# A two-layer diffusion block on one core: token tiles first in the queue, and a bias split into high and low part

## What is computed

```python
for l in range(DEPTH):                      # DEPTH = 2
    mod_l = split(silu(c) @ ada_w[l] + ada_b[l], 6)        # adaLN, latent; mod_c alike from c_ctx
    pl = modulate(rms_norm(xl, norm1_g[l]), mod_l[0], mod_l[1]) @ w_in[l]
    ml, mc = token_mixing(pl, pc, ...)      # pooling, neighbourhood attention, gMLP, latent attention
    xl = xl + mod_l[2] * (ml @ w_out[l])
    hl = modulate(rms_norm(xl, norm2_g[l]), mod_l[3], mod_l[4])
    xl = xl + mod_l[5] * grouped_moe(hl, ...)               # 16 experts, top 2
...
# neighbourhood attention
s_win = q . k * scale + bias                # bias from the learned table rpb, by row and column distance
s_win = where(valid, s_win, -1e30)
p = softmax(concat([s_win, s_ctx]))
```

## Time and profile before

| | us |
|---|---|
| runs: median of 3 (lowest, highest) | 913.67 (911.79, 914.56) |
| the profiled execution | 915.42 |
| its span, first to last instruction | 913.6 |
| TensorE busy, of the span | 836.8 |
| VectorE busy | 548.3 |
| ScalarE busy | 466.5 |
| GpSimd busy | 76.0 |

### The profile page before, as it was taken

One profiled execution on the slowest core, in us unless ns is written; L12 is line 12 of the kernel. 1 busy time (PEld: TensorE's weight loads), 2 busy tenths in 40 slices (PEclk: granted clock), 3 DMA queues, 4 the chain that ended last, 5 costly groups with the idle time before them and its releaser, 6 DMA issues. The chain is left out here.

```text
span 913.6 us, 15179 instructions
## 1 busy us (share of the span) xinstructions
PE 836.8 (92%) x6042; PEld 708.6 (78%) x6042; DVE 548.3 (60%) x807; ACT 466.5 (51%) x648; POOL 76.0 (8%) x103
## 2 busy tenths in 40 slices
PE   2989999999999789999999848999999799999985
PEld 2758967756787579999999835898669599999974
DVE  1263233249732777778778736662485668888854
ACT  1362221159721646566666525751673667676734
POOL 0103000520004000000000040302102000000000
PEclk9789999999999699999999975999999799999996
DMA  9796798984113037888988869952345159999901
GB/s 322 234 286 141 249 325 271 305 273 144 62 46 93 1 117 257 297 288 307 307 289 291 267 226 346 256 182 93 107 127 161 37 162 351 353 332 327 359 9 46
DMA packets 169122, 197.49 MB, mean 216 GB/s; under 512 B 15538, under 2 KB 156252, under 8 KB 169052
## 3 DMA queue, kind: packets, MB, share of 16 engines
q1 hardware_dynamic: 164400, 180.70, 62.4%
q10 hardware_dynamic: 3500, 11.64, 3.3%
q0 software_dynamic: 1152, 4.19, 1.4%
HBM read 187.09 MB, written 9.44 MB: 215 GB/s over the span
## 5 line engine op out<-in xcount | busy, mean ns | idle before, releaser
L2162 DVE TENSOR_TENSOR w_lo<-raw,w_hi 128x2048 fp32r<-128x2048 f32 x96 | 219.6, 2290 | 38.0 <-ACT w_hi L1071 37.4
L1071 ACT ACTIVATE w_hi<-raw 128x2048 fp32r<-128x2048 f32 x96 | 183.6, 1913 | 67.7 <-PE bank L1216 58.7
L1214 PE MATMUL bank<-w_hi,xg_hi 128*128 128x256 f32 x384 | 111.7, 291 | 3.1 <-DVE xg_lo L2323 2.5
L1215 PE MATMUL bank<-w_lo,xg_hi 128*128 128x256 f32 x384 | 109.3, 285 | 0.0
L1216 PE MATMUL bank<-w_hi,xg_lo 128*128 128x256 f32 x384 | 109.2, 284 | 0.0
L1214 PE MATMUL bank<-h_hi,w_hi 128*128 128x512 f32 (+2 forms) x288 | 103.9, 361 | 4.9 <-DVE h_lo L1934 4.0
L1215 PE MATMUL bank<-h_lo,w_hi 128*128 128x512 f32 (+2 forms) x288 | 101.5, 353 | 0.0
L1216 PE MATMUL bank<-h_hi,w_lo 128*128 128x512 f32 (+2 forms) x288 | 101.3, 352 | 0.0
L1214 PEld LDWEIGHTS bank<-w_hi,xg_hi 128*128 128x128 f32 x384 | 74.1, 193 | 3.4 <-issue 3.4
L1215 PEld LDWEIGHTS bank<-w_lo,xg_hi 128*128 128x128 f32 x384 | 74.4, 194 | 0.0
L1216 PEld LDWEIGHTS bank<-w_hi,xg_lo 128*128 128x128 f32 x384 | 74.2, 193 | 0.0
(11 more groups left out here) (302 smaller groups left out, 1598.2 us busy)
## 6 DMA issues: line engine op xcount, KB each, us to landing
raw<-in_ada_w SPq DMA_DIRECT2D x48, 1024.0 KB, 9.7
raw<-in_moe_w_gate SPq DMA_DIRECT2D x32, 1024.0 KB, 6.0
raw<-in_moe_w_up SPq DMA_DIRECT2D x32, 1024.0 KB, 6.3
raw<-in_moe_w_down SPq DMA_DIRECT2D x32, 1024.0 KB, 5.5
raw<-in_w_in SPq DMA_DIRECT2D x14, 1024.0 KB, 11.5
raw<-in_w_out SPq DMA_DIRECT2D x8, 1024.0 KB, 6.5
y_rows<-y_sb ACTq DMA_DIRECT2D x16, 512.0 KB, 4.8
na_bias<-in_na_rpb SPq DMA_DIRECT2D x4, 384.0 KB, 7.5
```

Of the source, the lines that this page charges most:

```text
L1071: act.activation(w_hi[slot][:, :, :], raw[q][:, :, :], ACT.Copy).then_inc(split_hi, 1)
L1214: pe.matmul(dst, w_hi_, x_hi_, start=first, stop=False)
L1215: pe.matmul(dst, w_hi_, x_lo_, start=False, stop=False)
L2162: dve.tensor_tensor(w_lo[slot][:, :, :], raw[q][:, :, :], w_hi[slot][:, :, :].bitcast(F32), ALU.subtract).then_inc(split_lo, 1)
```

## The change

Three things at the start, one in the attention.

1. The token tiles are issued by SyncE ahead of the first weight block. ScalarE's queue holds only the first constants, now 258 columns (identity, ones, epsilon), ahead of the vectors. Cosine and sine come with the other constants, later, in SyncE's queue; VectorE waits for these (`s_const`) before the first use.
2. The adaLN blocks with places 6 and 7 go to two buffers of their own, `ada_first`, in the room of `h_hi`, and don't wait for a slot.
3. The first modulation no longer stands ahead of the column sums, but between their two halves.
4. ScalarE copies the reversing matrix to fp32r (`flip`) and `na_bias` to its high part `bias_hi`, after block 6 of each layer. VectorE writes the low part `bias_lo` in the room of `na_bias`, ahead of block 7. TensorE adds the bias with two one-pass products, high and low part. `bias_hi` lies over `w_uq`, `w_uqs` and `sgu_wt`, so the copy waits for `s_go`. For this, `sgu_wt` moves ahead of `w_ukv`.

```diff
-N_FIRST = C_FLIP
+N_FIRST = C_COS
...
+        flip = sb("flip", [P, P], F32R)
+        bias_at = at[0]
         w_uq = sb("w_uq", [P, 2, HEADS * QK])
         w_uqs = sb("w_uqs", [P, 2, HEADS, ROPE])
+        sgu_wt = sb("sgu_wt", [P, 4, P])
         w_ukv = sb("w_ukv", [P, 4 * P])
         sgu_w_at = at[0]
         sgu_w = sb("sgu_w", [P, 4, P])
-        sgu_wt = sb("sgu_wt", [P, 4, P])
+        bias_hi = nc.alloc_sbuf_tensor_at("bias_hi", [P, HEADS, 6, GRID], F32R, offset=bias_at)
+        bias_lo = nc.alloc_sbuf_tensor_at("bias_lo", [P, HEADS, 6, GRID], F32R, offset=at[0])
         na_bias = sb("na_bias", [P, HEADS, 6, GRID])
...
+        ada_first = [nc.alloc_sbuf_tensor_at(f"ada_first{i}", [P, KC, BW], F32, offset=h_at + 4 * KC * BW * i) for i in range(2)]
...
+        def raw_of(l, r):
+
+            n = raw_index(l, r)
+            return ada_first[n - RAW] if RAW <= n < 8 else raw[n % RAW]
...
-                if p >= RAW:
+                if p >= (RAW if l else 8):
                     bl, br = ORDER[l][p - RAW]
...
-                sp.dma_start(raw[n % RAW][:, :, 0:w],
+                sp.dma_start(raw_of(bl, r)[:, :, 0:w],
...
+            for t in range(4):
+                sp.dma_start(x_tok[t][:, :], a["x" if t < 2 else "ctx"][(t % 2) * P:(t % 2 + 1) * P, :]).then_inc(s_xin, 16)
             for p in range(RAW):
                 load_block(0, p)
...
+            act.dma_start(const[:, 0:N_FIRST], a["const"][:, 0:N_FIRST]).then_inc(s_ident, 16)
             act.dma_start(raw_vec[0][0:112, :], a["vec0"]).then_inc(s_vecin, 16)
             act.dma_start(raw_vec[1][0:N_VEC - 112, :], a["vec1"]).then_inc(s_vecin, 16)
-            act.dma_start(const[:, 0:N_FIRST], a["const"][:, 0:N_FIRST]).then_inc(s_ident, 16)
-            for t in range(4):
-                act.dma_start(x_tok[t][:, :], a["x" if t < 2 else "ctx"][(t % 2) * P:(t % 2 + 1) * P, :]).then_inc(s_xin, 16)
...
+                    if n == 6:
+                        act.wait_ge(s_bias, 3 * l + 1)
+                        act.wait_ge(s_go, l + 1)
+                        act.activation(flip[:, :], const[:, C_FLIP:C_FLIP + P], ACT.Copy)
+                        act.activation(bias_hi[:, :, :, :], na_bias[:, :, :, :], ACT.Copy).then_inc(s_bias, 1)
...
                     for k in range(KC):
+                        if k == KC // 2:
+                            pe.wait_ge(s_cact, 1)
+                            modulate(0, bank[START_BANK[0]])
                         pe.wait_ge(n_sqa if k % 2 == 0 else n_sqd, k // 2 + 1)
...
-                    modulate(0, bank[START_BANK[0]])
...
-                            pe.matmul(dst[hd][:, 0:S], const[:, C_FLIP:C_FLIP + P],
-                                      na_bias[:, 2 * pair + hd, s:s + 4, :].rearrange("p r c -> p (r c)"),
-                                      start=False, stop=True, skip_group_check=True).then_inc(t_sc, 1)
+                            for part in (bias_hi, bias_lo):
+                                ins = pe.matmul(dst[hd][:, 0:S], flip[:, :], part[:, 2 * pair + hd, s:s + 4, :].rearrange("p r c -> p (r c)"),
+                                                start=False, stop=(part is bias_lo), skip_group_check=True)
+                            ins.then_inc(t_sc, 1)
...
-                pe.wait_ge(s_bias, l + 1)
+                pe.wait_ge(s_bias, 3 * l + 3)
...
+                    if n == 7:
+                        dve.wait_ge(s_bias, 3 * l + 2)
+                        dve.tensor_tensor(bias_lo[:, :, :, :], na_bias[:, :, :, :], bias_hi[:, :, :, :].bitcast(F32), ALU.subtract).then_inc(s_bias, 1)
...
                     if n == 1:
+                        if l == 0:
+                            dve.wait_ge(s_const, 16)
                         dve.tensor_copy(k_rope[rr, :], bank[3][0:ROPE, :])
```

More of the change, by code:

```diff
@@ L1242, in modulate @@
                     for g, (l, j) in enumerate(blocks):
-                        ins = pe.matmul(dst[32 * g:32 * g + 32, 0:BW], c_pad[:, k, :], raw[raw_index(l, j) % RAW][:, k, :],
+                        ins = pe.matmul(dst[32 * g:32 * g + 32, 0:BW], c_pad[:, k, :], raw_of(l, j)[:, k, :],
                                         start=(k == 0), stop=(k == KC - 1))
@@ L1321, in _ @@
             pe.transpose(bank[0][:, 112:N_VEC], raw_vec[1][0:N_VEC - 112, :], ident[0:N_VEC - 112, 0:N_VEC - 112]).then_inc(s_vt, 1)
-            pe.wait_ge(s_cact, 1)
             for l in range(DEPTH):
```

## The result

| | before | after |
|---|---|---|
| first comparison: median of 5 and 5 runs | 912.94 (911.12 to 914.56) | 908.83 (907.40 to 909.81) |
| the profiled execution | 915.42 | 908.22 |
| its span | 913.6 | 906.4 |
| its mean granted clock | 0.938 | 0.936 |

The ratio is 0.9939, with a 95% interval of 0.9914 to 0.9964. So the change makes the kernel faster, by 4.1 us in this comparison. Run twice more, beside other runs of the kernel before, the same kernel gave 0.9964 (0.9938 to 0.9989) and 0.9983 (0.9960 to 1.0005). Over all runs with their clock on record the mean is 913.6 +- 0.6 before (75 runs) and 910.4 +- 1.0 after (29 runs): 3.1 +- 1.1 us, which is 0.34%. The forecast was 7.9 us.

What follows compares the result with a forecast made beforehand. The prediction took TensorE to bound the kernel, with one large hole at the start. Start 5.6 plus bias 2.3 gave 7.9 us, from 913.67 to a median of 905.8, range 902.5 to 911.

Steps and rivals of the forecast that it cites:

- The start: 5.6 forecast: At the start, the first projection product comes at 45.1 instead of 50.76, shifting everything behind it by 5.6 us.
- The arrival of the blocks: Start transfers: eighth adaLN block usable at 32.9, first `w_in` block at 35.9, second at 37.8, 2.9 us earlier.
- The 1 us more that a faster queue was to give at best: Start transfers: a faster queue for 4 KB rows could add 1 us to the start's gain, making 6.6.
- the 0.4 us for the last of the 16 engines: Start transfers: 0.4 us added to each block's computed arrival until the last of the 16 engines is done.
- The first modulation: TensorE at the start: costed at the full clock, 3.66 us, starting after the fourth block at 20.8.
- the chain that I had ending at 36.6: TensorE's start at full clock: sums, both modulations and broadcast end at 36.6, so VectorE's 45.1 decides.
- The half-clock rival: TensorE's start at half clock from the fourth block ends at 44.5; total gain 3.6 us, time 910.1; chance 0.17.
- The bias: 2.3 forecast: Attention bias products: 0.39 us saved per job, counted in six of eight jobs, 2.3 us; bounds 0 and 3.1.
- the 0.1 for the switch: Attention bias group: 0.1 us for the switch, within the 0.74 us for four one-pass products.
- the softmax takes all of the bias gain: Attention: softmax absorbs the bias gain or conversions stand in the way; only the start gains, 908.1; chance 0.15.
- the early tiles bring only what the queue brings: Start: first product follows the second `w_in` block, 2.9 us earlier, and the bias gain is lost; 910.8; chance 0.09.
- Slower: Phases like the router's or between layers: half-clock stretches cost about 6.5 us each, two give 918.8; chance 0.04.

Runs made afterwards that it cites:

- start_only: The changed kernel's edits at the start, with the bias in one fp32 product as in the kernel before; 911.08 us, ratio 0.9969 to the kernel before.
- bias_only: The kernel before with the bias in high and low part, its start left as it was; 911.73 us, ratio 0.9991.
- tiles_only: The kernel before with only the token tiles ahead of the weights and the small first constants; 913.37 us, ratio 0.9998.
- dense_sums: The changed kernel with the start's sum of squares by eight one-pass products with a ones matrix, first modulation behind all sums; 912.01 us (one run).

## Why the prediction was right in direction and too large

**Right.** The kernel is faster, the median 908.83 lies in the range (902.5 to 911.0), and the steps could be found: tiles turned from 10.2 (forecast 9.1), a bias group of 0.73 (0.74), conversions hidden, a longer wait for the block in layer 0, nothing lost by the late cosine tables. The size is 3.1 to 4.8 us, not 7.9. That the first median lies in the range owes something to the width of the range and to luck: that comparison gave 4.1, the next two 4.4 and 1.2, and 908.83 is nearer to two of the rivals (908.1 and 910.1) than to 905.8. The prediction also named a sign of being wrong, half-clock stretches behind the first product that differ by more than 3.4 us in sum, and in the profiled pair they do: 13.6 us before and 3.4 us after up to the first attention job, then 17 against 23.9 in the router phase.

**The start: 5.6 forecast, about 2.8 found** (mean first product 49.6 in the two traces with the old start, 46.8 in the six with the new). Three terms were off.

- *The arrival of the blocks.* I had the eighth at 32.9 and the first `w_in` block at 35.9; they came at 34.3 and 37.3. The bytes were right: the first 15 us moved 4.71 MB where 4.61 was forecast (0.209 x 5 + 0.366 x 10), and nearly all of the 12.4 MB had moved by 37.0, against 37.4 forecast. The 1 us more that a faster queue was to give at best has no row behind it; the queue moved 383 GB/s in 5 to 10 us, as before, and 348 in 10 to 15. The term that was mis-sized is the 0.4 us for the last of the 16 engines. Behind 37.0 the transfers run on at a small share of the engines (0.13 up to 39.0), and GpSimd starts on the second `w_in` block at 39.02, where 37.8 was forecast:

```profile
37.00:39.00 2.00, 2.00 (x21) 0.99 (x24) 0.00 (x0) 1.73 (x1) 0.00 (x0) 0.50 0.13 40
```

What makes a few engines late is not shown. In the middle of the queue it looks alike: by 34.3 about 0.7 MB more had moved than had landed. The late block moved the end of the low part from 40.2 to 41.6, 1.4 us. Everything behind that low part took the forecast 4.9 us: in the third trace of the changed kernel VectorE goes from it to the modulation at 41.40, and the first product is at 46.30.
- *The first modulation.* I took 3.66 for it, since dense work had brought the full clock back before. It took 6.55, 6.3 and 5.0 in the three traces, behind sums of one column: TensorE was busy without a gap from 19.2 to 29.5 and stayed at half, so that dense work brings the clock back at once does not hold here. In two of them the chain that I had ending at 36.6 ended at 42.0 and 42.5, and TensorE, not VectorE, was last: 0.7 to 1.2 us. It is the same in start_only (47.48); in the other three traces with this start (46.30, 46.38, 46.35) the low part was last. The half-clock rival was half right in its mechanism; its 44.5 was too late, since the sums began at 17.8 beside the wait for blocks and the clock came back at 39.7.
- *The kernel before.* I took its one trace, 50.76, as its start. The same start gave 48.44 in bias_only, where TensorE began turning 0.7 us earlier and the half-clock stretch was shorter: the second modulation took 4.07 there and 4.76 in the trace before. A single trace's start is uncertain by 2 us, half of what was to be forecast.

**The bias: 2.3 forecast, about 1.56 found.** The saving for each job was right to 0.01; the 0.1 for the switch, for which the prediction names no row, shows in the first `bias_hi` product, 0.38 instead of 0.28. The step that failed is the count of jobs in which it reaches the end: I had six of eight, and 1.56 / 0.39 is four. The two at the block were left out already, and were lost as forecast. The saving of two more, 0.78, went to ScalarE, whose `prob_t` copy is next late. I had looked at VectorE's wait ahead of the maximum, 1.24 us, and not at ScalarE behind it.

**Given back behind both.** What TensorE gains ahead of a transfer-bound block is lost: the changed kernel came to the modulation of layer 0 8.55 ahead of the trace before and began it 7.68 ahead, so 0.87 was given back. At equal half-clock time the change is worth 4.8 us; 5 us more at half clock take 1.6 of it, which leaves about 3.1. bias_only shows the same (118 against 113 us), start_only does not (114). That would make the bias products, or the shorter jobs, the cause; with intervals of 3 us for each this is a hint and not shown. One place where it could come from is the modulation in layer 0: with the new bias products it ran at half in four of eight traces, at 5.2 to 5.4 us instead of 3.66, and in none of three with the old.

**The other rivals.** That the softmax takes all of the bias gain: no, a third of it. That the early tiles bring only what the queue brings (2.9 us): tiles_only, which leaves out the other edits, comes closest, with 1.1 +- 1.9. Slower: no; but the router's stretch at half was 23.9 or 27.3 us instead of 17 in most traces, with either start (bias_only: 27.3), so it is not the change's doing as far as one trace of the kernel before can tell.

## What to carry to other kernels

Before an edit at the start is priced, write down for each engine when its chain could end, and price TensorE's at both clock levels: two bounds 0.5 us apart (here the sums and modulations on TensorE, and the low part on VectorE) mean that an edit that removes one of them is worth only the difference. An idle stretch on TensorE that a transfer causes can be filled with products that nobody reads, and where the work behind it is dense this can pay: here 3.66 instead of 5.8 us for the next modulation. Where single executions scatter by 9 us, a pair of traces proves nothing by its total; compare offsets inside a phase.

## What was not expected of the hardware

- Two traces of one kernel (the changed one) had the first half of the one-column sums in 5.77 and 3.73 us, and the same modulation of 64 instructions in 6.55 and 4.98. Which stretches of the start run at half differs between executions of one program; what decides it was not found. The granted clock reads 1.00 up to its first entry in both, yet the turning instructions of the third trace start 5 to 7 in a us up to 13.7 and 10 or 11 in a us from there on; so the record is no guide to the clock ahead of that entry.
- A modulation behind 5.09 us of idleness took 5.57, behind 0.6 us 4.98, behind 1.0 us 3.66, behind 1.7 us 5.35: the length of the gap just ahead alone does not tell it.
- The reciprocal of 128x512 on VectorE takes 3.35 us, against 0.69 for a product of that size; it was hidden in dense_sums only because blocks were still on their way.
- The low part of the bias (128x1536, a subtraction on VectorE) took 2.52 in layer 0 and 2.05 in layer 1, where 1.75 was forecast from the weights' low part; why it is longer was not tried.
